# Strassen's scheme for gate and up of two feed-forwards, in three rounds of units

## The reference

```python
def swiglu(x, w_gate, w_up, w_down):
    return (jax.nn.silu(x @ w_gate) * (x @ w_up)) @ w_down
...
        h = modulate(rmsnorm(x, g_ffn[l]), sh2, sc2)
        gate, up = jnp.split(h @ w_gate_up[l], 2, axis=-1)
        x = x + gt2[:, None, :] * ((jax.nn.silu(gate) * up) @ w_down[l])
...
        h = h + 0.5 * swiglu(rms_norm(h, ffn1_norm[l]), ffn1_w_gate[l], ffn1_w_up[l], ffn1_w_down[l])
...
        h = h + 0.5 * swiglu(rms_norm(h, ffn2_norm[l]), ffn2_w_gate[l], ffn2_w_up[l], ffn2_w_down[l])
```

## Time and profile before

| what | value |
|---|---|
| median of 3 runs | 1714.38 us |
| lowest and highest | 1712.38 and 1716.47 us |
| span of the profiled execution | 1712.4 us |
| TensorE busy, mean granted clock | 99% of the span, 0.997 |
| VectorE, ScalarE, GpSimd busy | 48%, 36%, 8% |
| instructions | 22979 |

### The profile page before, as it was taken

How to read it: one execution, slowest core, us unless ns; L and a number is a source line. 1 busy time by engine, 2 the same in 40 slices (tenths; PEclk the granted TensorE clock), 3 DMA queues, 4 the chain that set the end, 5 groups by cost and what they waited for, 6 DMA issues and landing times.

```text
span 1712.4 us, 22979 instructions
## 1 busy us (share of the span) xinstructions
PE 1690.3 (99%) x8175; PEld 1369.3 (80%) x8175; DVE 817.3 (48%) x1277; ACT 614.4 (36%) x1066; POOL 140.8 (8%) x149
## 2 busy tenths in 40 slices
PE   7999999999999999999999999999999999999998
PEld 5777688888888887888888887777888888888888
DVE  4888755443333344444444325765555444444332
ACT  3565644222223233222222222655543322223222
POOL 0120210000001140000001131011001100000000
PEclk9999999999999999999999999999999999999999
DMA  9743134433342334333343346122233333333332
GB/s 326 244 130 112 43 93 123 147 107 92 95 116 85 101 103 130 98 98 98 97 119 97 92 133 117 50 63 70 77 95 99 94 93 96 98 98 111 102 95 73
DMA packets 298929, 184.60 MB, mean 108 GB/s; under 512 B 14555, under 2 KB 285335, under 8 KB 298855
## 3 DMA queue, kind: packets, MB, share of 16 engines
q1 hardware_dynamic: 294112, 169.89, 33.1%
q0 software_dynamic: 4400, 13.82, 3.4%
q10 hardware_dynamic: 360, 0.13, 0.0%
HBM read 180.67 MB, written 6.36 MB: 109 GB/s over the span
## 4 chain that ended last, share of the span: by engine, by line
PE 93%; DVE 3%; ACT 2%; DMA 1%; issue 1%; DVEq 0%; ACTq 0%; SPq 0%
PE psum L567 29%; PE psum L569 28%; PE psum L568 28%; PE psum L996 1%; PE psum L961 1%; PE psum L773 1%; PE psum L1016 1%; PE psum L733 1%; DMA w_raw<-in_ffn_w_gate 1%; PE psum L749 1%; DVE w_lo L1641 1%; DVE p L1794 0%; ACT p L1289 0%; PE psum L654 0%; DMA ident<-in_k_ident 0%
## 5 line engine op out<-in xcount | busy, mean ns | idle before, releaser
L567 PE MATMUL psum<-h_hi,w_hi 128*128 128x512 f32 x1480 | 586.4, 396 | 4.6 <-DVE w_lo L1641 2.8
L569 PE MATMUL psum<-h_hi,w_lo 128*128 128x512 f32 x1480 | 576.7, 390 | 0.0
L568 PE MATMUL psum<-h_lo,w_hi 128*128 128x512 f32 x1480 | 576.6, 390 | 0.0
L1641 DVE TENSOR_TENSOR w_lo<-w_raw,w_hi 128x1024 fp32r<-128x1024 f32 (+2 forms) x266 | 348.6, 1311 | 305.0 <-ACT w_hi L1229 301.2
L1229 ACT ACTIVATE w_hi<-w_raw 128x1024 fp32r<-128x1024 f32 (+2 forms) x266 | 288.2, 1084 | 165.0 <-PE psum L569 153.4
L567 PEld LDWEIGHTS psum<-h_hi,w_hi 128*128 128x128 f32 x1480 | 277.9, 188 | 85.3 <-issue 23.9
L569 PEld LDWEIGHTS psum<-h_hi,w_lo 128*128 128x128 f32 x1480 | 277.9, 188 | 59.3
L568 PEld LDWEIGHTS psum<-h_lo,w_hi 128*128 128x128 f32 x1480 | 278.1, 188 | 55.9 <-issue 1.0
L567 PE MATMUL psum<-hid_hi,w_hi 128*128 128x512 f32 (+1 forms) x550 | 209.6, 381 | 0.0
L569 PE MATMUL psum<-hid_hi,w_lo 128*128 128x512 f32 (+1 forms) x550 | 209.3, 381 | 0.0
L568 PE MATMUL psum<-hid_lo,w_hi 128*128 128x512 f32 (+1 forms) x550 | 209.3, 381 | 0.0
(11 more groups left out here) (266 smaller groups left out, 1383.5 us busy)
## 6 DMA issues: line engine op xcount, KB each, us to landing
w_raw<-in_w_in SPq DMA_DIRECT2D x50, 512.0 KB, 3.7
w_raw<-in_w_gate_up SPq DMA_DIRECT2D x44, 512.0 KB, 3.7
w_raw<-in_ffn_w_gate SPq DMA_DIRECT2D x44, 512.0 KB, 3.7
w_raw<-in_ffn_w_up SPq DMA_DIRECT2D x44, 512.0 KB, 3.6
w_raw<-in_ffn_w_down SPq DMA_DIRECT2D x32, 704.0 KB, 4.5
w_raw<-in_w_down SPq DMA_DIRECT2D x16, 704.0 KB, 4.5
sq<-in_w_ada SPq DMA_DIRECT2D x20, 512.0 KB, 4.9
ada_w<-in_w_ada SPq DMA_DIRECT2D x16, 512.0 KB, 10.9
```

The source lines that it names most:

```text
L567: pe.matmul(o, a_hi, b_hi, start=start, stop=False)
L568: pe.matmul(o, a_hi, b_lo, start=False, stop=False)
L569: return pe.matmul(o, a_lo, b_hi, start=False, stop=stop)
L1641: dve.tensor_tensor(w_lo[:, s % 2, 0:n], w_raw[:, s % 2, 0:n], w_hi[:, s % 2, 0:n].bitcast(F32), ALU.subtract).then_inc(w_ready, 1)
```

## The change

For feed-forwards 1 and 2, two hidden tiles (256 columns of gate and the same 256 of up) make a unit, 11 units in all. The matrix [gate up] of a unit is cut into 2 by 2 blocks, along the 1024 input channels (halves of 4 tiles) and between gate and up; h is cut along the channels and along the tokens (halves of 256). Strassen's scheme, in Winograd's form, gets the four results from 7 products of blocks. For that it needs four sums of weight blocks, T1 to T4, and four sums of blocks of h.

- TensorE: a unit is 7 products (`P1 Q5 P6 P2 P7 Q4 Q3`) of 24 matmuls on 256 tokens, 168 in all, where two tiles took 96 matmuls on 512 tokens. P2 is done in two parts around P7. Between products TensorE waits for copies of partial sums out of PSUM (`s1_set`, `u2_set`, `u3_set`, `c22_set`).
- Weights: 5 blocks of 512 KB per unit are loaded (one block of up twice), and 7 blocks are split: B11, T1, T2, T3, B21, T4, B22. The split blocks stand in a ring of 4 slots. Both engines split a block 4 places ahead of the product just done (`high_after`, `low_after`).
- VectorE: after the split of B11, T1, T2 and T3 it adds, in place, the sum that is the next T. It gets gate and up out of PSUM (`first_gate`, `second_gate`, `first_up`, `second_up`), and the hidden tiles (`hidden`, `hidden_low`), 512 elements each.
- ScalarE: the upper parts of 7 blocks, three copies out of PSUM (s1, u2, u3), SiLU twice, the upper part of the hidden tiles twice.
- The hidden dimension is done in 3 rounds: units 0 to 3, 4 to 6 and 7 to 10, each followed by its share of all 8 output tiles (8, 6 and 8 hidden tiles deep), added to x. Feed-forward 0 keeps the plain products but takes the same rounds and the ring.
- Ahead of feed-forwards 1 and 2, the last down (or `w_out`) goes in the order 0 4 1 5 2 6 3 7, and each tile of x is made into 2 or 5 blocks of h (`take_h`, `combos`, `parts_high`) in place of one h_hi and h_lo. VectorE does the first splits and sums of the next feed-forward among them.
- `rs_half` is gone; its factor 0.5 is in the instruction that reads PSUM.

```diff
+ROUNDS = [(0, 4), (4, 7), (7, KU)]
+PAIRED = [0, 4, 1, 5, 2, 6, 3, 7]
+SUMS = ["T1", "T2", "T3", "T4"]
...
+                    for name, n, done_ in (("B11", 0, "P1"), ("T1", 1, "Q5"), ("T2", 1, "P6"), ("T3", 2, "P7"),
+                                           ("B21", 4, "P2"), ("T4", 1, "Q4"), ("B22", 3, "Q3")):
+                        split_at((name, f, u), slot_no % 4, (set_, n), (done_, f, u))
...
+            def unit(f, u, sums, spreads):
...
+                product(y, "B11", A11, f, u, first=True, ready=None if q0 is None else q0 + 1).then_inc(f_prod, 1)
...
+                product(z, "T1", R1, f, u, first=True, ready=None if q0 is None else q0 + 2).then_inc(f_prod, 1)
...
+                await_item(("T2", f, u))
+                pe.wait_ge(s1_set, m)
+                product(y, "T2", R2, f, u).then_inc(f_prod, 1)
+                await_item(("B21", f, u))
+                x_ = take(("X", f, u))
+                product(x_, "B21", A12, f, u, (0,), first=True).then_inc(f_prod, 1)
+                pe.wait_ge(u2_set, m)
+                product(y, "T3", R3, f, u).then_inc(f_prod, 1)
+                product(x_, "B21", A12, f, u, (1,)).then_inc(f_prod, 1)
...
+                await_item(("T4", f, u))
+                pe.wait_ge(u3_set, m)
+                product(y, "T4", A22, f, u).then_inc(f_prod, 1)
+                await_item(("B22", f, u))
+                pe.wait_ge(c22_set, m)
+                product(z, "B22", R4, f, u).then_inc(f_prod, 1)
...
+            def high(r):
+
+                key, slot, s_, b = in_ring[r]
+                if key[0] in SUMS:
+                    act.wait_ge(f_added, 4 * pair_count[key[1:]] - 3 + SUMS.index(key[0]))
+                else:
+                    act.wait_ge(part_landed[s_][b], 16 * raw_count[key])
+                if ring_free[key] is not None:
+                    act.wait_ge(f_prod, prod[ring_free[key]])
...
+                act.activation(ring_hi[slot][:, 0:n], pool_raw[s_][b][:, 0:n], ACT.Identity).then_inc(f_high, 1)
...
+                if m > 1:
+                    act.wait_ge(c11_set, m - 1)
...
+                act.activation(s1, psum[:, y, :], ACT.Copy).then_inc(s1_set, 1)
...
+            def lower(r):
+
+                key, slot, s_, b = in_ring[r]
+                dve.wait_ge(f_high, r + 1)
...
+                dve.tensor_tensor(ring_lo[slot][:, 0:n], raw_[:, 0:n], ring_hi[slot][:, 0:n].bitcast(F32),
+                                  ALU.subtract).then_inc(f_ready, 1)
+                if key[0] in ("B11", "T1", "T2", "T3"):
...
+                    dve.wait_ge(f_ready, r + 1)
...
+                    dve.tensor_tensor(raw_[:, :], raw_[:, :], pool_raw[o_set][o_b][:, :], ALU.add).then_inc(f_added, 1)
...
+            def combos(n, name):
...
+                    done(part(H1, H21, H22, ALU.subtract))
+                    done(part(H2, H1, H11, ALU.subtract))
+                    part(H4, H12, H2, ALU.add).then_inc(combos_set, 1)
```

More of the change, by code:

```diff
@@ new lines, in downs @@
+            def downs(f, r, between=None):
+                ks, order = range(2 * ROUNDS[r][0], 2 * ROUNDS[r][1]), downs_of(f, r)
+                down_part(f, r, order[0], ks[:-2], True)
+                down_part(f, r, order[1], ks[:-2])
+                down_part(f, r, order[0], ks[-2:], True)
+                down_part(f, r, order[1], ks[-2:])
+                if between is not None:
+                    between()
+                for n in order[2:]:
+                    if not (f == 2 and r == len(ROUNDS) - 1 and n == KD - 1):
+                        down_part(f, r, n, ks)
@@ L895, in spreads_ffn1 @@
+            def ffn(f, sums, spreads):
+                for r in range(len(ROUNDS)):
+                    for u in units_of(r):
+                        unit(f, u, sums, spreads)
+                    downs(f, r)
+            plain_ffn()
             def spreads_ffn1():
@@ L1472, in last_block, with ffn @@
+            def ffn(f, scales, down):
+                for r in range(len(ROUNDS)):
+                    for u in units_of(r):
+                        unit(f, u, r, scales)
+                    downs(f, r, down if r == len(ROUNDS) - 1 else None)
             def last_block():
@@ L1953, in down0, with downs @@
-            def down0(n, i):
-                add_gated(("down", 0), "down0", n, i, GT2)
-                next_low("down0", GEN["ffn1"], n, i, gff[:, slot_of(n, i, 2)])
-            ffn(0, lambda: None, lambda: mod_group(GT2 // KD, KD), down0)
-            def scale_ffn1():
+            lower(2)
+            lower(3)
+            def downs(f, r, down):
+                for i, n in enumerate(downs_of(f, r)):
+                    last = f == 2 and r == len(ROUNDS) - 1
+                    if not (last and n == KD - 1):
+                        down(r, i, n)
```

829 lines of the change are left out of this document (579 added, 250 removed).

## The result

The change makes the kernel slower: 1817.6 us (median of 4 runs, 1815.6 to 1821.4) against 1715.2 us of the kernel before, run beside it, a ratio of 1.060 (95% interval 1.0585 to 1.062). The forecast was 1781 us with a range up to 1808: the direction was right, the size was not, by 37 us.

What follows compares the result with a forecast made beforehand. The prediction took TensorE, busy 99% of the span, as the bound. To a 1712.4 us span it added 45.2 for units, 16, 4 and 2 elsewhere: 1779.6, so 1781 us measured; range 1758 to 1805, widened to 1745 to 1808.

Steps and rivals of the forecast that it cites:

- What TensorE saves: Units of feed-forwards 1 and 2: 20.16 us of TensorE for 21.76 before, 35.2 us less over 22 units.
- What a unit adds: VectorE and ScalarE wait in turn: first unit 21.0 us, middle 25.1, last 24.2; feed-forwards 1 and 2 take 45.2 us more.
- The walk: Step through a unit's engine queues in order with prices and hand-overs, giving 25.2 us for a unit in a full queue.
- Between the parts: Work on x tiles ahead of feed-forwards 1 and 2 makes TensorE wait: 16 us, with smaller terms of 4 and 2.
- 4 for units 0 and 1: In units 0 and 1 of each feed-forward, the scale's chain and SiLU table fall into the full queue: 4 us.
- 2 for feed-forward 0 and the tail: Feed-forward 0 waits for modulation columns with two PSUM banks for downs; the tail has shorter halves: 2 us.
- more than 25 us lost there: Sign of being wrong: more than 25 us lost between the parts.
- GpSimd: Ahead of feed-forwards 1 and 2, GpSimd's adds slow VectorE by 0.9 us a tile with two adds: 5.5 us in all.
- The split of `w_out`: Ahead of feed-forward 2, TensorE waits for the w_out slab's split: 14.9 us a pair of tiles, 8.3 us in all.
- TensorE stays the bound: Rival: both queues run beside each other, units take 20.16 us, only work between the parts costs: 1697 us; 10%.
- Only VectorE's work and Q3: Rival: waits in units are short, only VectorE's work and the wait before Q3 count: units of 21.0 us, 1720 us; 8%.
- The forecast's own bounds on a hand-over: Gaps between engines in a unit range from 0.03 to 0.23 us, making a full-queue unit 24.8 to 27.2 us.

Runs made afterwards that it cites:

- e2: The change with VectorE's queue reordered: sum of T3 beside T1's upper part, combinations from PSUM earlier; unit 0's first_gate takes the old scale; 1730.9 us.
- e13: e12 with ScalarE's squares behind its upper parts and, ahead of feed-forward 1, VectorE's lower parts of a tile behind the next tile's addition; 1705.9 us.
- e3: The change with GpSimd adding only one of 512 columns of each square in feed-forward 0's last downs and the output tiles (wrong norms); 1794.8 us, one run.
- e4: The change with the first two slabs of the projection after feed-forward 1 split ahead of the last down's addition on both engines; 1806.9 us.
- e12: e6 with T1's split back among the x tiles and the split of a w_out slab one tile earlier on both engines; 1710.0 us.
- e6: e5 and e4 together, with three splits moved behind the last x tile and a w_out slab's upper part no longer waiting for GpSimd; 1719.1 us.
- e7: e6 with the light GpSimd adds of e3; 1703.2 us, one run.
- e11: e6 with T1's split back among the x tiles and the last two tiles' squares sent to TensorE directly, not through GpSimd's adds; 1722.6 us.
- e10: The change with only first_gate (except in unit 0) and first_up moved earlier in VectorE's queue, the sums left in place; 1758.1 us.
- e5: e2 with first_gate of unit 0 put back behind the copy of the new token scale; 1727.0 us.

## Why the prediction was wrong

**What TensorE saves** held. The step inside a product is 0.120 us, and e2 shows units of 20.16 us from end to end, 1.60 less than the 21.76 before. That all 35.2 us can be had is not shown: e13, the best version, is 6.6 us under the kernel before.

**What a unit adds** held: 21.0, 25.1 and 24.2 us forecast, 21.0, 25.2 to 25.7 and 24.2 to 24.8 measured, with the waits where they were said to be (1.13 before the splits of T2 and T3, 2.95 for s1 before P6, 0.63 for c22 before Q3; the one for u2 before P7 stands in some units alone). Unit by unit that is 8 us too little over both feed-forwards. The walk kept TensorE at full clock through its own waits. The three units that stay at full clock behind the gap of 3.2 us take 25.16, 24.19 and 24.18 us, the forecast's 25.1 and 24.2; the others lose 1.1 to 1.4 us at half clock there, of which the next wait swallows all but 0.4 to 0.6. The prices of sums (1.23) and copies out of PSUM (0.60) were right.

**Between the parts** is the step that failed: the forecast had 16 us, 4 for units 0 and 1, and 2 for feed-forward 0 and the tail, 22 in all. Measured are 4.2 in feed-forward 0, 20.4 and 7.7 beyond 21.0 us in the two units 0, 12.7 in the output tiles and 7.2 after feed-forward 1, 52.2 in all. That is 30 of the 34 us by which the profiled span exceeds the forecast's, and the prediction itself named more than 25 us lost there as a sign of being wrong. Most terms had their mechanism right and their size wrong; the queue past the last down and the half clock had no term. The parts, some of which overlap:

- *GpSimd.* The forecast took 0.9 us for each tile with two adds, 5.5 in all, from a split that went from 1.63 to 2.57, beside the one add that stands there, and counted four tiles. A tile has two adds, each costs up to 1.05, and all eight tiles have them: by estimate 17 us, and 8 for the output tiles with one add each, 25 at most; e3 measures 18.4. The row was read as the price of a tile and was that of an add.
- *The queue past the last down.* The two first splits for the projection stand behind the last down's addition; the forecast didn't look there at all. 7 us (e4).
- *The split of `w_out`.* The forecast named it, and priced it by the sum of work per pair of tiles (14.9 us against 10.88; two pairs of 4.0 are 8.0, where it says 8.3). What counts is its place: behind the parts of the tile before. Moved one tile ahead it costs 7.3 us less in the stretch and 2.8 more in the unit behind it (e12), with the same sum.
- *Half clock.* Unit 0 of feed-forward 1 has 45 slow steps, 4.2 us, that of 2 has 27, 2.5 us; no term had them. e3 removes 4.5 of these 6.7 us with the adds, so they count in part twice.

What stays open: how the 17.5 us by which unit 0 of feed-forward 1 in e13 still exceeds 21.0 divide between the chain of the last x tile, GpSimd and the half clock (37 slow steps, 3.5 us). Between e6 and e7 6.5 of 15.4 went with GpSimd's adds; a version with its adds elsewhere at no price was not found (e11 shows none).

**The rivals.** "TensorE stays the bound" decided at a middle unit under 21 us. It was no rival for this order of the queues, but e12 and e13, whose units are 20.16 us, are that case: 1710 and 1706 us, against its 1697. "Only VectorE's work and Q3" gave 21.0 us a unit; e10 is nearest, at 21.8. The forecast's own bounds on a hand-over (up to 27.2 us a unit) held, and did not help, since the error lay elsewhere.

## What to carry to other kernels

Two engines that share out a chain of short steps can leave a third waiting while neither is full: look at who is idle for whom in the timeline, and put independent work of one between its result and its next need of the other. Here that alone was worth some 90 of 102 us (e5), with no instruction less. Where a fast stage begins, walk each queue from the last tile of the stage before, GpSimd's included, as carefully as the steady state; the sum of work over a stretch says little about it.
